# Placing and spreading the maximum units of a prompt attention's groups

## The chip, the cores and the metric

The kernel runs on one core of one Trainium2 chip. The metric is the device time of one execution in microseconds (us); the time before is the median of three runs. Engines are named as in the profile: PE is TensorE's matmuls and PEld its weight loads, DVE is VectorE, ACT is ScalarE, POOL is GpSimd, SP is SyncE, which issues most transfers.

## The reference, cut to what matters

One decoder step: projections, a paged decode attention over eight sequences, a causal prompt attention over 4096 tokens with 8 heads of 64, gates with a pooling mixer, and an output projection. What the change touches is the prompt attention:

```python
s = einsum('bqhd,bkhd->bhqk', q, k) * ATTN_SCALE
s = s + (fq[..., :, None] - fk[..., None, :])       # cumulative log-forget of query and key
s = where(k_pos[None, :] <= q_pos[:, None], s, -inf)
p = softmax(s, axis=-1)
out = einsum('bhqk,bkhd->bqhd', p, v)
```

The softmax needs the maximum of each query's row before the first exponential of that row.

## The kernel before, in words

The kernel is five phases, one behind the other: projection, decode attention, prompt attention (`phase_attend`, from 1037 to 2422 us of the profiled execution), gates, merge. The change is in `phase_attend` alone.

**Blocks and quads.** Queries are cut into tiles of 512. A block b is one head (b // 8) with one query tile (row(b) = b % 8), 64 blocks in all. Block b has row(b) + 1 quads; a quad is 512 keys against the 512 queries of the block, and the last quad of a block lies on the diagonal. There are 288 quads. A quad is two steps; a step is 256 keys: its scores are written by `scores(s, half)` in two halves, each of two matmuls (L1149, L1150), and a third small one that adds the mask on the diagonal (L1153), where the columns also narrow from 512 to 384, 256 and 128. ACT takes the exponentials of a step (`exps`, L985; on the diagonal L989, two instructions), POOL adds the probabilities up for the denominator (L951, L952, L932, L954 to L957), and PE multiplies them with v (`weigh`, L1170).

**Groups.** Three quads make a group, so there are 96 groups (numbered 0 to 95 here) of six steps and twelve halves. For each group PE's program runs the twelve halves of scores with maximum units between them, then `spread_shift` (L1130) for the blocks that start in the next group, then the six `weigh` steps (the weighing), then `total` (L1184), the denominators of blocks that ended in the group before. The score tensor `st` holds two steps, so `scores(s)` waits until the exponentials of step s - 2 are done (L1143). PE executes its program strictly in order.

**Maximum units.** The maxima are found ahead of the scores by matmuls of their own. A unit is 128 queries against up to 512 keys: one matmul (L1122) with 512 columns, or 128 to 512 on the diagonal, into one of the two banks of `mx`, then one reduction by DVE (L1048, or L1044 with the mask on the diagonal). There are 1152 units. Bank n % 2 is used again only when DVE has finished the use n - 2 (`bank_free`, L1105). When all units of a block are reduced, DVE combines them (`combine`, L1055), PE spreads the result (L1130), and ACT copies it (L967) where the scores of the block read it. DVE's order in a group is: the units that the blocks starting in the next group need, their `combine`, the other units of the group, the joins of POOL's partial sums (L1062), the denominators' copies (L1073).

**The plan.** `units_by[g]` is how many units have been issued by the end of group g. It is planned backwards from the last group: no fewer than the blocks that start in group g + 1 need plus `LATE` = 2, and no fewer than the next group's number minus `most_units(g + 1)`. `EARLY` = 14 units are issued ahead of group 0. `units_after(g, place)` says which units follow which half: place 0 is ahead of the first half, place p behind half p, so place 12 is behind the last half. In the kernel before, a group takes at most 13 units (one at each place), or 12 from group 12 on where one of its quads is on the diagonal (one at each of the places 1 to 12). The plan of before is: group 0 has 28 units, two or three at a place; 44 groups have 13; 41 have 12; the groups 9, 21, 33, ... 81 have 5 to 7; the last three groups have none.

The lines to follow are 711 to 733 (the plan), 1105 to 1124 (bank and unit on PE), 1133 to 1155 (scores), 1195 to 1211 (the order on PE), 1038 to 1048 and 1081 to 1094 (DVE's side).

```python
def bank_free(n):
    if n >= 2:
        pe.wait_ge(bank_done, n - 1)
```

Of the kernel before, what the change touches and what calls it, by code (L numbers as in the profile page):

```python
# [36 lines left out]
NT = SEQ // TILE  # L37
# [627 lines left out]
def phase_attend(nc, io, keep):  # L665
# [5 lines left out]
    LATE = 2  # L671
    QUADS = 3
    STEPS = 2 * QUADS
# [13 lines left out]
    def row(b):  # L687
        return b % NT

    quad_base = [sum(row(a) + 1 for a in range(b)) for b in range(NB + 1)]  # L690
# [7 lines left out]
    NGROUP = NQUAD // QUADS  # L698
# [3 lines left out]
    def on_diagonal(n):  # L702
        return n + 1 == quad_base[block_of[n] + 1]

    def starting(g):
        return [b for b in range(NB) if start_group[b] == g]
# [2 lines left out]
        return [b for b in range(NB) if end_group[b] == g]  # L709

    def most_units(g):
        return 4 * QUADS if g >= quad_base[NT] // QUADS and any(on_diagonal(QUADS * g + i) for i in range(QUADS)) else 4 * QUADS + 1

    units_by = [0] * NGROUP
    for g in reversed(range(NGROUP)):
        if starting(g + 1):
            units_by[g] = unit_base[starting(g + 1)[-1] + 1] + LATE
        if g + 1 < NGROUP:
            units_by[g] = max(units_by[g], units_by[g + 1] - most_units(g + 1))
        units_by[g] = min(units_by[g], unit_base[NB])  # L720
    EARLY = unit_base[starting(0)[-1] + 1] + LATE
    assert EARLY >= unit_base[starting(0)[-1] + 1]

    def units_in(g):
        return range(units_by[g - 1] if g else EARLY, units_by[g])

    def units_after(g, place):

        units = units_in(g)
        if len(units) > 2 * STEPS:  # L730
            return units[place * len(units) // (2 * STEPS + 1):(place + 1) * len(units) // (2 * STEPS + 1)]
        places = [1 + i * 2 * STEPS // len(units) for i in range(len(units))]
        return [k for k, p in zip(units, places) if p == place]

    def unit_at(k):
# [23 lines left out]

    bank_uses = [("unit", k) for k in range(EARLY)]  # L760
    for g in range(NGROUP):
# [9 lines left out]
    with ExitStack() as ctx:  # L771
# [243 lines left out]
        def _(dve):  # L1015
# [22 lines left out]
            def unit(k):  # L1038
                b, t, c = unit_at(k)
                n = bank_of["unit", k]  # L1040
                width = TILE if c < row(b) else (t + 1) * P
                dve.wait_ge(bank_ready, n + 1)
                if c == row(b):
                    nc.vector.tensor_tensor_reduce(out=mx[:, n % 2, 0:width], in0=mx[:, n % 2, 0:width], in1=tri[:, TILE - width:TILE], scale=1.0,  # L1044
                                                   scalar=NO_MAX, op0=ALU.add, op1=ALU.max,
                                                   accum_out=max_parts[:, b % AHEAD, t, c:c + 1]).then_inc(bank_done, 1)
                    return
                nc.vector.tensor_reduce(max_parts[:, b % AHEAD, t, c:c + 1], mx[:, n % 2, 0:width], AX_X, ALU.max).then_inc(bank_done, 1)  # L1048

            def combine(b):  # L1050
                h, j = head(b), row(b)
                dve.wait_ge(bank_done, bank_of["unit", unit_base[b + 1] - 1] + 1)
                if b >= 2:
                    dve.wait_ge(shift_spread, b - 1)
                nc.vector.tensor_reduce(shift_w[:, b % 2, :, HD], max_parts[:, b % AHEAD, :, 0:j + 1], AX_X, ALU.max, negate=True).then_inc(shift_ready, 1)  # L1055
# [19 lines left out]
            for b in starting(0):  # L1075
                for k in range(unit_base[b], unit_base[b + 1]):
                    unit(k)
                combine(b)
            for k in range(unit_base[starting(0)[-1] + 1], EARLY):
                unit(k)  # L1080
# [19 lines left out]
        def _(pe):  # L1100
# [9 lines left out]
            def unit(k):  # L1110
                b, t, c = unit_at(k)
                h, j = head(b), row(b)
                if k == unit_base[b]:
                    pe.wait_ge(q_loaded[b % AHEAD], (b // AHEAD + 1) * 80)
                    if j == 0 and h:
                        pe.wait_ge(bias_loaded[h % 2], (h + 1) // 2 * 16)
                    if j % 2 == 0 and h:
                        pe.wait_ge(k_loaded[h % 2][j // 2], (h + 1) // 2 * 48)
                n = bank_of["unit", k]
                bank_free(n)  # L1120
                width = TILE if c < j else (t + 1) * P
                last = nc.tensor.matmul(mx[:, n % 2, 0:width], q_top[0:KM, b % AHEAD, t * P:(t + 1) * P],  # L1122
                                        k_one[h % 2][0:KM, c * TILE:c * TILE + width], start=True, stop=True)
                last.then_inc(bank_ready, 1)
# [64 lines left out]
            pe.wait_ge(keep["k_first"], 16 * FIRST_LOADS)  # L1189
            for k in range(EARLY):  # L1190
                unit(k)
# [3 lines left out]
            for g in range(NGROUP):  # L1195
                for k in units_after(g, 0):
                    unit(k)
                for place in range(2 * STEPS):
                    scores(STEPS * g + place // 2, place % 2)
                    for k in units_after(g, place + 1):  # L1200
                        unit(k)
                if starting(g + 1):
                    pe.wait_ge(exp_done, STEPS * g + STEPS - 1)
                for b in starting(g + 1):
                    spread_shift(b, starting(g + 1)[0])
                for s in range(STEPS * g, STEPS * g + STEPS):
                    weigh(s)
                for b in dens_after(g):
                    total(b)
# [1171 lines left out]
def build(nc, io):  # L2381
    with ExitStack() as ctx:
        m = Alloc(nc, ctx, "keep")
        keep = {
            "ident": m.sb("ident", [P, P]),
            "ones": m.sb("ones", [P, P]),
            "hs_high": m.sb("hs_high", [P, KC, NS], F32R),
            "hs_low": m.sb("hs_low", [P, KC, NS], F32R),
            "f_tot": m.sb("f_tot", [H, NT]),
            "k_first": m.sem("k_first"),  # L2390
            "w_first": [m.sem("w_first0"), m.sem("w_first1")],
            "h_first": m.sem("h_first"),
            "mix_first": m.sem("mix_first"),
        }
        lane_a = nc.sbuf_base
        lane_b = lane_a + SEQ * 4
        m.sb("lanes", [P, 2 * SEQ])
        for name, lane, dt in (("project_high", lane_a, F32R), ("project_low", lane_b, F32R),
                               ("key_one", lane_a, F32R), ("key_all", lane_b, F32R),
                               ("gate_raw", lane_a, F32), ("gate_tokens", lane_b, F32), ("gate_high", lane_a, F32R),  # L2400
                               ("mix_raw", lane_b, F32), ("out_raw", lane_a, F32)):
            keep[name] = nc.alloc_sbuf_tensor_at(f"keep_{name}", [P, SEQ], dt, offset=lane)
        phase_project(nc, io, keep)
        phase_decode(nc, io, keep)
        phase_attend(nc, io, keep)
        keep["mix_s"] = m.sb("mix_s", [NS, D])
        phase_gates(nc, io, keep)
        phase_merge(nc, io, keep)
# [34 lines left out]
```

## Time and profile before

| what | value |
|---|---|
| median of three runs | 3414.8 us (3410.24 to 3417.29) |
| time of the profiled execution | 3415.05 us |
| its span in the trace | 3413.5 us |
| mean granted TensorE clock | 0.97 of full speed |
| PE matmul busy | 3228.7 us (95% of the span) |
| PE weight loads busy | 2309.1 us (68%) |
| DVE busy | 1744.9 us (51%) |
| POOL busy | 1382.8 us (41%) |
| ACT busy | 1125.5 us (33%) |

An engine's busy time is the time in which at least one of its instructions was open. Matmuls overlap in the profile: one with 512 columns is shown as 0.40 us long, while the next begins 0.23 us after it. What a matmul costs in a row of matmuls is therefore read from start to start, not from its duration. The text gives times in us from the start of the span.

### The profile page before, as it was taken

To read this page: it belongs to the slowest core of one execution; us is meant where nothing else is said; L and a number is where in the kernel's file an instruction comes from. 1 tells how busy PE (TensorE), PEld (TensorE's weight loads), DVE (VectorE), ACT (ScalarE), POOL (GpSimd) and SP (SyncE) were. 2 spreads that over 40 slices of the span, in tenths; PEclk is the share of its full clock that TensorE was granted. 3 is DMA by queue.
4 is the path that set the end of the run, shared out by engine and by line. 5 is a ranking of instruction groups with operands and counts; after the bars stand their busy time and mean duration, and the time that the engine had idled before them with its cause. 6 is when DMAs were issued, how large, how long until landed. Compare 5 with 4: busy or idle time off the path is not lost. (4 is left out here: it accounts for less than half of the span.)

```text
span 3413.5 us, 47511 instructions
## 1 busy us (share of the span) xinstructions
PE 3228.7 (95%) x16720; PEld 2309.1 (68%) x16720; DVE 1744.9 (51%) x2947; ACT 1125.5 (33%) x1536; POOL 1382.8 (41%) x1273
## 2 busy tenths in 40 slices
PE   8999999796978999999999999999799999979998
PEld 5888777672725666666666666666488888858886
DVE  4333333361515766666666666666344433554544
ACT  4222222241312555545555555554411211111011
POOL 1000000234333888888888888888500000000000
PEclk9999999897987999999999999999999999989999
DMA  5333443599996123222232323220211121167664
GB/s 183 136 137 133 142 167 120 203 358 379 366 378 138 29 53 73 60 66 60 66 66 60 70 56 70 57 80 10 96 50 51 60 86 49 49 179 218 198 203 147
DMA packets 240077, 435.55 MB, mean 128 GB/s; under 512 B 63588, under 2 KB 107717, under 8 KB 237804
## 3 DMA queue, kind: packets, MB, share of 16 engines
q1 hardware_dynamic: 216395, 358.40, 34.5%
q0 software_dynamic: 20768, 68.17, 5.2%
q10 hardware_dynamic: 2742, 6.81, 0.7%
q8 instruction: 93, 1.52, 0.2%
q14 instruction: 79, 0.65, 0.1%
HBM read 314.39 MB, written 119.08 MB: 127 GB/s over the span
## 5 line engine op out<-in xcount | busy, mean ns | idle before, releaser
L1048 DVE TENSOR_REDUCE at_max_parts<-at_mx 128x1 f32<-128x512 f32 x896 | 612.6, 691 | 165.9 <-PE at_mx L1122 151.9
L985 ACT ACTIVATE at_probs<-at_st,at_gap 128x1024 f32<-128x1024 f32 x448 | 498.4, 1115 | 376.4 <-PE at_st L1150 375.7
L951 POOL TENSOR_TENSOR at_pair_sum<-at_probs 128x1024 f32<-128x1024 f32 x224 | 537.4, 2399 | 140.9 <-ACT at_probs L985 119.0
L1170 PE MATMUL at_o_ps<-at_probs,at_v 128*64 128x512 f32 (+3 forms) x2304 | 490.6, 564 | 0.0
L1170 PEld LDWEIGHTS at_o_ps<-at_probs,at_v 128*64 128x64 f32 x2304 | 179.6, 137 | 261.7 <-issue 220.8
L952 POOL TENSOR_TENSOR at_quad_sum<-at_pair_sum 128x512 f32<-128x512 f32 x224 | 305.7, 1365 | 17.6
L93 PE MATMUL ga_acc<-keep_gate_high,ga_w_high 128*128 128x512 f32 x768 | 299.1, 389 | 0.0
L95 PE MATMUL ga_acc<-keep_gate_high,ga_w_low 128*128 128x512 f32 x768 | 299.0, 389 | 0.0
L94 PE MATMUL ga_acc<-ga_h_low,ga_w_high 128*128 128x512 f32 x768 | 298.9, 389 | 0.0
L1122 PE MATMUL at_mx<-keep_key_one,at_q_top 71*128 71x512 f32 (+2 forms) x576 | 236.2, 416 | 10.2 <-DMA at_q_one<-scratch_q_parts 5.9
L1711 POOL MEMSET mg_minus_half<- 128x1 f32 x1 | 0.6, 612 | 569.8 <-POOLq L66 569.8
L93 PE MATMUL mg_acc<-mg_w_high,mg_mix_high 128*128 128x512 f32 x512 | 202.6, 396 | 29.8 <-DVE mg_w_low L1766 23.1
L1122 PE MATMUL at_mx<-at_k_one,at_q_top 71*128 71x512 f32 (+2 forms) x576 | 227.9, 396 | 0.9 <-DVE at_den_out L1073 0.8
L1149 PE MATMUL at_st<-at_q_all,keep_key_all 128*128 128x512 f32 (+1 forms) x576 | 225.0, 391 | 1.6 <-ACT at_probs L989 0.8
L1149 PE MATMUL at_st<-at_q_all,at_k_all 128*128 128x512 f32 (+1 forms) x576 | 224.2, 389 | 2.4 <-ACT at_probs L985 1.2
L1150 PE MATMUL at_st<-at_q_one,keep_key_one 67*128 67x512 f32 (+1 forms) x576 | 221.6, 385 | 0.0
L1150 PE MATMUL at_st<-at_q_one,at_k_one 67*128 67x512 f32 (+1 forms) x576 | 219.2, 381 | 0.0
L300 POOL TENSOR_TENSOR pj_rms<-pj_squares,pj_eps_sum 128x1 f32<-128x1 f32 (+1 forms) x33 | 7.4, 224 | 491.4 <-ACT pj_junk L318 479.6
L93 PE MATMUL pj_acc<-keep_project_high,pj_w_high 128*128 128x512 f32 x512 | 202.9, 396 | 1.1 <-DVE pj_kv_rows L463 0.8
L94 PE MATMUL mg_acc<-mg_w_low,mg_mix_high 128*128 128x512 f32 x512 | 201.2, 393 | 0.0
L95 PE MATMUL mg_acc<-mg_w_high,mg_mix_low 128*128 128x512 f32 x512 | 201.1, 393 | 0.0
L95 PE MATMUL pj_acc<-keep_project_high,pj_w_low 128*128 128x512 f32 x512 | 199.6, 390 | 0.0
(337 smaller groups left out, 5734.8 us busy)
## 6 DMA issues: line engine op xcount, KB each, us to landing
dc_pages<-in_cache_k_dram SPq DMA_DIRECT2D x128, 256.0 KB, 10.7
dc_pages<-in_cache_k_dram POOLq DMA_DIRECT2D x128, 256.0 KB, 6.1
dc_pages<-in_cache_v_dram SPq DMA_DIRECT2D x128, 256.0 KB, 8.9
dc_pages<-in_cache_v_dram POOLq DMA_DIRECT2D x128, 256.0 KB, 5.5
scratch_h_t<-pj_h_t SPq DMA_DIRECT2D x8, 2048.0 KB
scratch_q_parts<-pj_stage SPq DMA_DIRECT2D x32, 512.0 KB, 3.4
scratch_k_parts<-pj_stage SPq DMA_DIRECT2D x32, 512.0 KB, 2.7
scratch_attn_t<-at_o_out SPq DMA_DIRECT2D x128, 128.0 KB, 2.4
```

What stands on the lines that cost most here:

```text
L93: nc.tensor.matmul(out, lhs_high, rhs_high, start=first, stop=False)
L94: nc.tensor.matmul(out, lhs_high, rhs_low, start=False, stop=False)
L95: return nc.tensor.matmul(out, lhs_low, rhs_high, start=False, stop=last)
L300: chain.link(nc.gpsimd.tensor_tensor(out, squares[0:rows, n:n + 1], eps_sum[0:rows], ALU.add))
L951: chain.link(nc.gpsimd.tensor_tensor(pair, first, second, ALU.add))
L952: end(n, nc.gpsimd.tensor_tensor(out, pair[:, 0], pair[:, 1], ALU.add))
L985: nc.scalar.activation(probs[:, s % RING], st[:, s % 2], ACT.Exp, bias=bias).then_inc(exp_done, 1)
L1048: nc.vector.tensor_reduce(max_parts[:, b % AHEAD, t, c:c + 1], mx[:, n % 2, 0:width], AX_X, ALU.max).then_inc(bank_done, 1)
L1122: last = nc.tensor.matmul(mx[:, n % 2, 0:width], q_top[0:KM, b % AHEAD, t * P:(t + 1) * P], k_one[h % 2][0:KM, c * TILE:c * TILE + width], ...
L1149: nc.tensor.matmul(out, k_all[h % 2][:, keys], q_all[:, b % AHEAD, at:TILE], start=True, stop=False)
L1150: last = nc.tensor.matmul(out, k_one[h % 2][0:KR, keys], q_one[0:KR, b % AHEAD, at:TILE], start=False, stop=(c < j))
L1170: last = nc.tensor.matmul(o_ps[half * HD:(half + 1) * HD, b % 2, at:TILE], v[:, h % 2, 4 * c + own], probs[:, s % RING, half, at:TILE], st ...
```

## The change

`most_units` is 14 for every group, whatever lies on the diagonal. The plan is no longer allowed to fall from one group to the next, so groups behind the last unit have none. In `units_after`, the last two units of a group (`LATE`) are put at place 12, behind the last half of the scores; the others are spread over the places from 1 on, one at a place, and only a group with more than 14 units uses the old rule.

```diff
     def most_units(g):
-        return 4 * QUADS if g >= quad_base[NT] // QUADS and any(on_diagonal(QUADS * g + i) for i in range(QUADS)) else 4 * QUADS + 1
+        return 4 * QUADS + 2

     units_by = [0] * NGROUP
     for g in reversed(range(NGROUP)):
...
         units_by[g] = min(units_by[g], unit_base[NB])
+    for g in range(1, NGROUP):
+        units_by[g] = max(units_by[g], units_by[g - 1])
     EARLY = unit_base[starting(0)[-1] + 1] + LATE
...
         units = units_in(g)
-        if len(units) > 2 * STEPS:
-            return units[place * len(units) // (2 * STEPS + 1):(place + 1) * len(units) // (2 * STEPS + 1)]
-        places = [1 + i * 2 * STEPS // len(units) for i in range(len(units))]
+        last = 2 * STEPS
+        spread = len(units) - LATE
+        if spread > last:
+            return units[place * len(units) // (last + 1):(place + 1) * len(units) // (last + 1)]
+        places = [1 + i * last // max(spread, 1) for i in range(spread)] + [last] * LATE
         return [k for k, p in zip(units, places) if p == place]
```

Worked out from these lines, the plan is now: `EARLY` stays 14; group 0 has 20 units (one or two at a place); 77 groups have 14, one at each of the places 1 to 11 and three at place 12; group 87 has 12, two of them at place 12; the groups 9, 21, 33, 45, 57, 69 and 81 have none; the groups behind these (10, 22, ... 82) have four, at the places 1, 6, 12 and 12; groups 93 to 95 have none, as before. The number of units and of all other instructions is the same.

## Rows read from the trace of the kernel before

**Rows 1.** The page: busy time of the engines over the whole span.
```profile
PE 3228.7 (95%) x16720; PEld 2309.1 (68%) x16720; DVE 1744.9 (51%) x2947; ACT 1125.5 (33%) x1536; POOL 1382.8 (41%) x1273
```
**Rows 2.** Busy by stretch: length, busy us (instructions) per engine, PEclk, DMA share, GB/s.
```profile
1400.00:1600.00 200.00, 199.50 (x1028) 129.94 (x1028) 135.69 (x248) 106.37 (x135) 173.79 (x128) 1.00 0.28 65
```
**Rows 3.** Waits from 900 to 2400 us: engine line <- releaser: us, times, longest.
```profile
ACT at_probs L985 <- PE at_st L1150: 369.8, 430, 6.4
...
POOL at_pair_sum L951 <- ACT at_probs L985: 118.9, 84, 9.1
...
PEld at_mx L1122 <- DVE at_max_parts L1048: 20.7, 95, 1.0
```
**Rows 4.** Timeline of group 31, one half: start, us, engine, line, tiles, count.
```profile
1511.05 1.39 DVE L1048 TENSOR_REDUCE at_max_parts<-at_mx 128x1 f32<-128x512 f32 x2
...
1511.32 0.40 PE L1122 MATMUL at_mx<-keep_key_one,at_q_top 71*128 71x512 f32 x1
...
1512.02 0.39 PE L1122 MATMUL at_mx<-keep_key_one,at_q_top 71*128 71x512 f32 x1
```
**Rows 5.** Timeline on PE, end of group 31, weighing, total, begin of group 32.
```profile
1516.13 0.40 PE L1122 MATMUL at_mx<-keep_key_one,at_q_top 71*128 71x512 f32 x1
1516.46 5.37 PE L1170 MATMUL at_o_ps<-at_probs,at_v 128*64 128x512 f32 x24
1521.76 0.42 PE L1184 MATMUL at_mx<-at_quad_sum,keep_ones 128*32 128x128 f32 x8
1522.12 0.50 PE L1122 MATMUL at_mx<-keep_key_one,at_q_top 71*128 71x512 f32 x1
1522.45 0.40 PE L1149 MATMUL at_st<-at_q_all,keep_key_all 128*128 128x512 f32 x1
```
**Rows 6.** Timeline, end of group 30, whose last quad is on the diagonal.
```profile
1501.50 1.29 DVE L1048 TENSOR_REDUCE at_max_parts<-at_mx 128x1 f32<-128x512 f32 x2
1501.61 0.45 PE L1122 MATMUL at_mx<-keep_key_one,at_q_top 71*128 71x512 f32 x1
...
1502.07 0.27 PE L1153 MATMUL at_st<-at_tri_t,at_ident_r 128*128 128x128 f32 x1
...
1502.25 0.33 PE L1122 MATMUL at_mx<-keep_key_one,at_q_top 71*128 71x128 f32 x1
```
**Rows 7.** Timeline, end of group 92: its last unit is needed by the spread.
```profile
2368.99 0.40 PE L1122 MATMUL at_mx<-at_k_one,at_q_top 71*128 71x512 f32 x1
...
2369.43 0.70 DVE L1044 CUSTOM_DVE_ANT_0 at_mx<-at_mx,at_tri 128x512 f32<-128x512 f32 x1
2370.05 0.14 DVE L1044 DVE_READ_ACCUMULATOR2_ANT at_max_parts<- 128x1 f32 x1
...
2370.55 0.43 PE L1130 MATMUL at_st<-at_ident_r,at_shift_w 128*65 128x128 f32 x4 [1.17 <-DVE at_shift_w L1055]
```
**Rows 8.** Stretches of groups 21, 22, 93 and 94, columns as in rows 2.
```profile
1368.50:1381.18 12.68, 12.54 (x61) 7.79 (x59) 7.54 (x13) 6.84 (x9) 11.97 (x10) 1.00 0.09 21
1381.18:1395.39 14.21, 14.21 (x70) 8.39 (x70) 9.86 (x19) 6.68 (x6) 13.01 (x9) 1.00 0.16 38
...
2376.22:2388.21 11.99, 11.07 (x54) 6.70 (x52) 1.38 (x2) 6.62 (x9) 11.24 (x10) 1.00 0.10 23
2388.21:2400.84 12.63, 12.15 (x58) 5.95 (x57) 0.00 (x0) 6.36 (x6) 11.93 (x8) 1.00 0.00 0
```
**Rows 9.** Timeline on ACT, group 94: two exponentials a row.
```profile
2389.46 2.12 ACT L985 ACTIVATE at_probs<-at_st,at_gap 128x1024 f32<-128x1024 f32 x2 [3.96 <-PE at_st L1150]
2391.88 2.12 ACT L985 ACTIVATE at_probs<-at_st,at_gap 128x1024 f32<-128x1024 f32 x2 [0.30 <-PE at_st L1150]
```
**Rows 10.** Stretches of group 0: scores part and weighing, columns as in rows 2.
```profile
1055.69:1079.40 23.71, 22.86 (x64) 16.86 (x64) 16.85 (x35) 6.11 (x10) 7.72 (x9) 0.50 1.00 196
1079.40:1086.50 7.10, 7.10 (x25) 3.45 (x24) 0.42 (x2) 1.18 (x2) 2.04 (x3) 0.62 0.71 157
```
**Rows 11.** Timeline on PE, group 0: units behind each other.
```profile
1066.81 0.79 PE L1122 MATMUL at_mx<-keep_key_one,at_q_top 71*128 71x512 f32 x1 [0.65 <-DVE at_max_parts L1048]
...
1067.83 0.63 PE L1150 MATMUL at_st<-at_q_one,keep_key_one 67*128 67x512 f32 x1
...
1068.26 0.63 PE L1122 MATMUL at_mx<-keep_key_one,at_q_top 71*128 71x512 f32 x1
```

## The prediction

> **What bounds the kernel now.** The page's busy shares come first: PE is open for 95% of the span, no other engine for more than 51% [rows 1]. The stretches show what that means in the prompt attention: from 1400 to 1600 us PE is busy for 199.5 of 200 us at a granted clock of 1.00, POOL for 174, DVE for 136, ACT for 106 [rows 2]. The waits agree: ACT waits for scores (369.8 us), POOL waits for ACT (118.9 us), while PE's waits for DVE's reductions are 20.7 us in 95 places [rows 3]. So PE's order and its own waits set the time, every microsecond that PE stands still in this phase is a microsecond of the kernel, and slack on DVE or POOL is worth nothing by itself.
>
> The margin is thin in one place. In group 31 a unit starts every 0.70 us on PE (1511.32, 1512.02), which is two matmuls of scores and one unit at 0.234 each; DVE's two reductions there take 1.39 us, 0.695 each [rows 4]. A unit that comes once per half is just kept up with. Behind the group's last unit (1516.13) the weighing starts 0.33 later and lasts to 1521.76 [rows 5]; DVE has no units in that time.
>
> **The change, part by part.** No instruction is added or removed. Units move: 8 out of group 0, and out of the groups 9, 21, ... and 10, 22, ...; 77 groups now have 14. In these, three units stand behind each other at place 12.
>
> *The three units in a row.* Let T be the start of the first. The unit before it started at T - 0.70. DVE takes a unit up 0.44 behind its start (2368.99 to 2369.43 [rows 7]), so it reduces that one from T - 0.26 to T + 0.43. The second unit needs that bank. PE starts a waiting unit 0.06 behind the end of the reduction: in group 30 the first of two reductions ends near 1502.19 (half a pair of 1.29, its own length being 0.69), and the unit starts at 1502.25, where the mask's matmul before it began at 1502.07 and takes 0.06 [rows 6]. So the second unit starts at T + 0.49 instead of T + 0.23: 0.25 lost. The third needs the bank of the first, which is reduced from T + 0.44 to T + 1.13: it starts at T + 1.19, instead of 0.23 behind the second: 0.48 lost. Together 0.73 per group. Nothing covers this, since the weighing, which would not need these banks, is queued behind the units on PE. 77 x 0.73 = 56.2, and 0.25 in group 87 with its two: **+56.5**. The bounds: 0 if the wait were hidden in some way that the rows do not show, and 0.9 per group if DVE comes late to T. A part of the units is narrow (the mean is 469 of 512 columns), which takes a little off.
>
> *DVE late at the diagonal.* In 38 of the 77 groups the last quad is on the diagonal, halves are shorter than a reduction there, and DVE is already behind when place 12 comes: the units at 1501.61 and 1502.25 are 0.64 apart, and the second of them had waited [rows 6]. Between 0 and 0.2 each; the few hundredths by which that unit was late are the nearest, 0.07 x 38 = **+2.7**.
>
> *The spread.* Where a starting block needs all but two units of the group, its last needed unit is now the first of the three. From such a unit to the spread it takes 1.56 us (2368.99 to 2370.55, with a reduction on the diagonal of 0.76) [rows 7]; the third unit starts near T + 1.25 there and is over by T + 1.4 to 1.5, so the spread waits for 0.1 to 0.2 more. This is so in 16 groups; in 8 of them the plan of before ended as tight and waited already, elsewhere the need had been met long before. **+2**, between 0 and 4.
>
> *Groups with few units.* Without units, scores outrun ACT. In group 94, which has none, exponentials start every 1.21 us (two in 2.42: 2389.46 to 2391.88 [rows 9]), and PE needs four matmuls, 0.94, for a step; from the third step on PE waits about 0.27 each. Units that stood there ran for free. Groups 9, 21, ... 81 get none: group 93, of the same shape, takes 11.99 where group 21 takes 12.68 with seven units of 2816 columns [rows 8], which are 1.29 of matmul time; the units gone should have saved 1.29 and save 0.69, a loss of 0.60. Groups 10, 22, ... 82 keep four of 13, of which one stands where it fills a wait (place 6), one comes ahead of the second half and delays the first exponentials, and two come last: 4 x 0.27 - 0.23 = 0.85 lost, where group 22 has no such waits (PE busy 14.21 of 14.21 [rows 8]). 7 x (0.60 + 0.85) = **+10.1**. Between 5 and 14.
>
> *Place 0.* A unit ahead of the first half is gone. The first matmul behind the weighing takes 0.33 to the next one, a unit or not (1522.12 to 1522.45 [rows 5]; the weighing starts likewise 0.33 behind the last unit). No gain: 0.
>
> *Group 0.* It loses 8 units (3968 columns), which are paid later at the full clock with 3968 x 0.234 / 512 = **+1.8**. The scores part of group 0 takes 23.71 us at a clock of 0.50, the lower level of 1.2 GHz, and the weighing 7.10 at 0.62 [rows 10]; there a matmul of 512 columns costs 0.43 (1067.83 to 1068.26), and the second of two units waits for DVE (the one at 1066.81: 0.65 idle) [rows 11]. Eight units less are 8 x 0.41 = 3.3, and most of the waits between doubled units go, about 1.9: 5.2 less. But the clock rises inside the weighing. If it rises at the same moment as before, the work that moves ahead of it runs at half speed, and only half of 5.2 is kept; if it rises at the same place of the program, all. **-3.5**; bounds -2.6 and, if a PE with fewer gaps got the full clock from group 0's begin on (23.7 to about 14 us for 20 reductions), -12.
>
> *Cover.* The joins on DVE (1.6 us, at most two) start some 0.1 us later relative to the weighing and still end inside it. SP's loads of q and k wait on scores and on groups that are all later, and need no more room. Other phases are not touched.
>
> The sum: 56.5 + 2.7 + 2 + 10.1 + 1.8 - 3.5 = 69.6, on the profiled execution's 3415.05 (span 3413.5 and 1.5 around it; 0.25 over the median): **3484.5 us**, 2% more.
>
> **What a page says of the clock.** In group 92 PE stood idle for 1.17 us ahead of the spread [rows 7], and the stretches behind it (groups 93, 94) still have a granted clock of 1.00 [rows 8]; so I put no loss of clock into the sum. The Trainium skill (TensorE: Matmul & The Clock Gate, "A second HAM failure mode: psum-queue depth-cycling") says that a PE which micro-idles between groups of matmuls while it cycles through PSUM banks can swing between the two clock levels. That speaks against this change, which adds such a gap to 77 groups; by that rule the time would be that of the clock rival below, the trace with its one gap does not agree, and it has no repeated gaps to show.
>
> **The rivals.**
> - *The clock falls at the gaps.* For it: the gap comes back every 15 us, and group 0, with its waits for DVE, never got the full clock in its scores part. Against it: group 92. Price: a matmul costs 0.43 instead of 0.234 [rows 11], 13 us of such a group would take 11 us more; if one in ten of the 77 groups were hit, 85 us more, 3570.
> - *The wait is partly covered.* If DVE came to the first of the three earlier than I read, or narrow units were luckier, half of 56.5 is lost: 3456.
> - *Faster.* The mechanism is DVE's lead at the diagonal. In before, some 47 of the 96 groups have diagonal halves shorter than a reduction, and PE waits for DVE inside them [rows 6]; a group that begins with scores and whose doubled units lie in front of the weighing would keep DVE ahead, if the last two units cost PE nothing. It decides at place 12: the waits must be absent there. Then at most the 20.7 us of waits [rows 3] go, and group 0 gives 3.5: 3391. Against it: two banks, and 0.69 for each reduction.
> - *Nothing to see.* If POOL set the pace (174 of 200 us), PE's waits would be absorbed, and ACT's loss too: 3415. Against it: POOL itself waits for ACT.
>
> **How the numbers follow.** The forecast has 0.82, the partly covered wait 0.06, the clock 0.06, faster 0.03, nothing 0.03. The range takes the forecast's bounds (-12 for group 0 and some 14 off the three units below; 0.2 per diagonal group, 4 for the thin groups and a few short falls of the clock above) and reaches to the partly covered case: 3458 to 3500. A change of 0.2%, 6.8 us, is about what a measurement of this kernel can tell from none: faster 0.03, same 0.03, slower 0.94.
>
> **What would show it.** In the timeline on PE: three L1122 at the end of a group, 0.49 and 0.7 apart, and the weighing 1.5 behind the first. In the waits: PE or PEld at L1122 for DVE L1048 up from 20.7 to about 75 us. Groups 9, 21, ... near 12.0 us, groups 10, 22, ... near 13.3, groups with 14 units near 15.2 where 13 took 14.4. The clock at 1.00 from group 1 to the end of the phase. I am wrong if the three units stand 0.23 apart, or if the phase's stretches show a clock below 1.00.

## The result and the profile after

The changed kernel takes 3486.61 us (median of four runs, 3482.32 to 3490.21) beside 3413.49 of the kernel before (also four runs, 3410.24 to 3417.29): a ratio of 1.0211, interval 1.0199 to 1.0223, 2.1% slower. Forecast were 3484.5 and a range of 3458 to 3500. The profiled execution took 3490.21 us (span 3488.6), 75.2 more than that of before.

The busy line of the page stands beside [rows 1]:

```profile
PE 3272.3 (94%) x16720; PEld 2311.6 (66%) x16720; DVE 1734.0 (50%) x2947; ACT 1123.8 (32%) x1536; POOL 1382.6 (40%) x1273
```

PE is open for 43.6 us more with the same 16720 matmuls: two that overlap less are open longer, and that is no added work. Stretches of the changed kernel show more (columns as in [rows 2]). In order they are: the stretch of [rows 2]; the middle of the phase; the scores part and the weighing of group 0 ([rows 10]); groups 21 and 22 ([rows 8]); group 31, where a unit came every 0.70 us in [rows 4]; and group 93 ([rows 8]):

```profile
1400.00:1600.00 200.00, 195.25 (x966) 120.43 (x967) 125.37 (x232) 96.43 (x117) 167.57 (x120) 1.00 0.24 54
...
1100.00:2400.00 1300.00, 1267.14 (x6190) 783.03 (x6189) 820.77 (x1490) 629.34 (x757) 1068.12 (x760) 0.99 0.25 57
...
1053.51:1072.02 18.51, 18.51 (x56) 15.05 (x56) 11.46 (x25) 6.11 (x10) 6.77 (x8) 0.50 0.96 184
1072.02:1078.77 6.75, 6.75 (x26) 3.29 (x25) 0.53 (x1) 1.19 (x2) 2.98 (x4) 0.65 1.04 226
1381.63:1393.61 11.98, 11.06 (x54) 6.70 (x52) 0.83 (x1) 6.62 (x9) 11.25 (x10) 1.00 0.10 23
1393.61:1406.92 13.31, 13.03 (x62) 6.70 (x61) 4.13 (x8) 6.58 (x6) 12.31 (x9) 1.00 0.16 40
...
1527.88:1543.22 15.34, 15.06 (x72) 8.59 (x71) 12.13 (x18) 7.29 (x7) 12.57 (x9) 1.00 0.22 53
...
2449.27:2461.25 11.98, 11.06 (x55) 6.71 (x53) 1.39 (x2) 6.61 (x9) 8.37 (x8) 1.00 0.10 23
```

PE was busy for 199.5 of 200 us and now is for 195.25. Group 31 takes 15.34 us with 14 units. Group 21 has no units any more and takes what group 93 takes (11.98); group 22 takes 13.31. And from 1100 to 2400 us the granted clock is 0.99, not 1.00.

The waits from 900 to 2473 us of the changed kernel; the third line answers to the last of [rows 3], which was 20.7 us in 95 places:

```profile
ACT at_probs L989 <- PE at_st L1154: 365.0, 396, 7.4
POOL at_pair_sum L955 <- ACT at_probs L989: 173.6, 81, 7.5
...
PEld at_mx L1126 <- DVE at_max_parts L1052: 63.6, 161, 1.0
...
PE at_mx L1126 <- DVE at_max_parts L1052: 18.0, 72, 0.6
```

PE and PEld together wait 81.6 us for DVE's reductions at L1052, where the forecast had about 75. POOL waits for ACT for 173.6 us instead of 118.9: it has more slack now. The end of group 31, which answers to [rows 5], on PE, and then DVE's reductions of the same time:

```profile
1535.95 0.98 PE L1126 MATMUL at_mx<-keep_key_one,at_q_top 71*128 71x512 f32 x2
1537.13 0.50 PE L1126 MATMUL at_mx<-keep_key_one,at_q_top 71*128 71x512 f32 x1 [0.19 <-DVE at_max_parts L1052]
1537.56 5.37 PE L1174 MATMUL at_o_ps<-at_probs,at_v 128*64 128x512 f32 x24
...
1543.22 0.50 PE L1153 MATMUL at_st<-at_q_all,keep_key_all 128*128 128x512 f32 x1
```

```profile
1535.69 2.67 DVE L1052 TENSOR_REDUCE at_max_parts<-at_mx 128x1 f32<-128x512 f32 x4 [0.19 <-PE at_mx L1126]
1538.28 1.77 DVE L1066 TENSOR_TENSOR at_quad_sum<-at_quad_sum 128x512 f32<-128x512 f32 x1
```

The first row holds the first two of the three units. A matmul of 512 columns that follows a gap is shown 0.50 long, so the second began at 1535.95 + 0.98 - 0.50 = 1536.43, 0.48 behind the first. The third began at 1537.13, 1.18 behind the first, and DVE finished a reduction every 0.67 in that time. Without waits they would stand 0.23 apart. The idle time in brackets is only 0.19, because it counts from the modelled end of a matmul; the distance of the starts is what is lost. The weighing begins 0.43 behind the last unit, where [rows 5] had 0.33.

**The sum of the groups.** Taken from start to start, the 96 groups are 74.6 us longer in the profiled execution. What a group takes over its matmuls at 0.234 us for 512 columns is its excess. A thin group is one with no or only four units, and a fall is a short stretch in which the granted clock is at its lower level (shown further below). The parts are:

| part | forecast | measured |
|---|---|---|
| 77 groups of 14 and group 87: three in a row, diagonal, spread | 56.5 + 2.7 + 2 = 61.2 | 62.0 |
| 7 groups without units | 4.2 | 3.7 |
| 7 groups with four units | 5.9 | 7.4 |
| 8 units moved out of group 0 | 1.8 | 1.8, not measured apart |
| group 0 | -3.5 | -5.6 |
| falls of the clock in five weighings | 0 | 8.0 |
| ends of eight groups (-2.1) and the last group (-0.6) | 0 | -2.7 |
| sum | 69.6 | 74.6 |

### The profile page after: what moved, and what is told of

Its sections match the earlier page's. It is cut to its first block and busy times, and to the rows that moved or that the text cites. A ratio compares the mean times of both kernels' runs of the same rounds, so it can differ in the third digit from the quotient of the medians.

```text
span 3488.6 us, 47511 instructions
## 1 busy us (share of the span) xinstructions
PE 3272.3 (94%) x16720; PEld 2311.6 (66%) x16720; DVE 1734.0 (50%) x2947; ACT 1123.8 (32%) x1536; POOL 1382.6 (40%) x1273
## 5 line engine op out<-in xcount | busy, mean ns | idle before, releaser
L1052 DVE TENSOR_REDUCE at_max_parts<-at_mx 128x1 f32<-128x512 f32 x896 | 605.1, 690 | 178.9 <-PE at_mx L1126 169.8
L955 POOL TENSOR_TENSOR at_pair_sum<-at_probs 128x1024 f32<-128x1024 f32 x224 | 536.5, 2395 | 196.1 <-ACT at_probs L989 173.6
L1174 PE MATMUL at_o_ps<-at_probs,at_v 128*64 128x512 f32 (+3 forms) x2304 | 498.2, 572 | 0.0
L956 POOL TENSOR_TENSOR at_quad_sum<-at_pair_sum 128x512 f32<-128x512 f32 x224 | 294.3, 1314 | 17.6
L1126 PE MATMUL at_mx<-keep_key_one,at_q_top 71*128 71x512 f32 (+2 forms) x576 | 236.1, 418 | 20.4 <-DVE at_max_parts L1052 9.2
L1126 PE MATMUL at_mx<-at_k_one,at_q_top 71*128 71x512 f32 (+2 forms) x576 | 230.3, 404 | 13.5 <-DVE at_max_parts L1052 8.8
```

Of the source, the lines that this page charges most:

```text
L955: chain.link(nc.gpsimd.tensor_tensor(pair, first, second, ALU.add))
L956: end(n, nc.gpsimd.tensor_tensor(out, pair[:, 0], pair[:, 1], ALU.add))
L1174: last = nc.tensor.matmul(o_ps[half * HD:(half + 1) * HD, b % 2, at:TILE], v[:, h % 2, 4 * c + own], probs[:, s % RING, half, at:TILE], st ...
```

## The experiments

Theory A is the forecast's: PE waits for DVE's reduction of the bank two units back, and the weighing is queued behind. The kernel before was measured again beside them, with medians between 3415.9 and 3417.0 us.

**e1_old_places.** The new plan with the old places:

```diff
-        last = 2 * STEPS
-        spread = len(units) - LATE
-        if spread > last: ...
-        places = [1 + i * last // max(spread, 1) for i in range(spread)] + [last] * LATE
+        if len(units) > 2 * STEPS:
+            return units[place * len(units) // (2 * STEPS + 1):(place + 1) * len(units) // (2 * STEPS + 1)]
+        places = [1 + i * 2 * STEPS // len(units) for i in range(len(units))]
```

> The plan of the changed kernel (77 groups of 14 units), but with the places of before: one unit at each of the places 0 to 11 and two at place 12. Theory A (the cost is the wait for two banks at the end of a group): only the second unit of the pair waits, 0.25 us instead of 0.73, so the 77 groups lose some 19 us instead of 56 and the time is about 3487 - 37 = 3450 us, a few less if falls of the clock go as well (3438 to 3454). The thin groups stay as slow as in the changed kernel. Rival B (the cost is the plan itself, full groups and thin groups, wherever the units stand): the time stays within 8 us of 3487.

Measured: 3449.43 us, ratio 1.0093 (1.0072 to 1.0114). As theory A has it: half of the loss (37 us of 73) was where the units stood, with the counts of all groups unchanged. The rest is mainly the pair at place 12 (0.36 in each of 77 groups) and the thin groups (9 us).

**e2_old_plan.** The old plan with the new places:

```diff
     def most_units(g):
-        return 4 * QUADS + 2
+        return 4 * QUADS if g >= quad_base[NT] // QUADS and any(on_diagonal(QUADS * g + i) for i in range(QUADS)) else 4 * QUADS + 1
```

> The plan of before (12 and 13 units, group 0 with 28), but the new places: the last two units of a group at place 12, the others from place 1 on. Theory A: one wait of 0.25 us in 85 groups, 21 us, and a few for doubled places: 3414 + 24 = 3438 us (3432 to 3446). Rival B (the plan alone costs): within 6 us of 3414. With e1 this also says what the third unit at place 12 costs over the second: by theory A it is twice as dear (0.48 against 0.25).

Measured: 3449.46 us, ratio 1.0094 (1.0076 to 1.0111), 33 us over before and not 24; the range of 3432 to 3446 was missed. The places alone cost, so rival B is out, but each of the 85 groups lost 0.38 us and not 0.25. The missing 0.1 is read in the starts. A unit of 512 columns that had to wait is followed by the spread 0.34 us later, where it was 0.24 without a wait, and by the weighing 0.43 us later, where it was 0.33. The excess of the changed kernel's groups has this cost too, once for each group.

**e3_narrow_tail.** DVE's time alone, PE's program untouched. The two reductions that the last units wait for read 128 columns, so these maxima are over fewer keys:

```diff
+    narrow = {k for g in range(1, NGROUP) if len(units_in(g)) > 2 * STEPS for k in units_in(g)[-4:-2]}
...
                 width = TILE if c < row(b) else (t + 1) * P
+                at = width - P if k in narrow else 0
...
-                nc.vector.tensor_reduce(..., mx[:, n % 2, 0:width], AX_X, ALU.max)
+                nc.vector.tensor_reduce(..., mx[:, n % 2, at:width], AX_X, ALU.max)
```

> The changed kernel, but the two reductions for which the last two units of a group wait (the unit at place 11 and the first at place 12) read only the last 128 of their columns; the maximum of these units is then taken over fewer keys. PE's program is the same to the instruction. Theory A: the second unit no longer waits, the third waits from T + 0.47 to T + 0.44 + 0.29 + 0.06 = T + 0.79, 0.32 us; the tail costs 0.32 instead of 0.73, 77 x 0.41 = 32 us less: about 3455 us (3445 to 3462), with L1126's idle for DVE falling from 99 to about 67 us. Rival B (three matmuls into the same bank pair cost PE this however long DVE takes): 3487.

Measured: 3456.52 us, ratio 1.0119 (1.0101 to 1.0136), 30 less than the changed kernel. With the same order on PE and only DVE faster, the loss shrinks by about what the arithmetic of the three starts says: the groups with 14 units have 0.36 less excess each, where 0.41 was expected. The end of group 29 of this kernel on PE:

```profile
1493.28 0.62 PE L1129 MATMUL at_mx<-keep_key_one,at_q_top 71*128 71x512 f32 x2
1494.06 0.50 PE L1129 MATMUL at_mx<-keep_key_one,at_q_top 71*128 71x512 f32 x1 [0.16 <-DVE at_max_parts L1055]
```

The first two units now stand 0.23 apart, and the third is 0.78 behind the first; expected was 0.79. So the wait is for the reductions. PE's idle time at L1126 for them, diagonal ones included, fell from 99.3 to 59.2 us.

**e4_units_in_weighing.** The last two units behind the first step of the weighing, where both banks are free:

```diff
-        places = [...] + [last] * LATE
+        places = [...] + [last if needs_all(g) else last + 1] * LATE
...
                     weigh(s)
+                    if s == STEPS * g:
+                        for k in units_after(g, 2 * STEPS + 1):
+                            unit(k)
```

> The changed kernel, but the last two units of a group stand behind the first step of the weighing instead of at place 12 (group 92, where the spread needs all, stays as it is). The first step takes 0.88 us, so both banks are free when PE comes to them. Theory A: the tail's 56 us go, the diagonal's 3 and most of the falls of the clock too (8 us): 3487 - 65 = 3422 us (3415 to 3435, the upper end if DVE's joins, now some 2 us later in the weighing, hold up the totals). The thin groups keep their 11 us, group 0 its gain. Rival B: units cost what they cost, 3487. Rival C (a switch between the matmul kinds costs some 0.1 us each way, 0.2 per group): 3437.

Measured: 3473.03 us, ratio 1.0163 (1.0146 to 1.018). A clear miss, by 51 us. On PE, the end of group 14 of this kernel:

```profile
1284.57 0.43 PE L1139 MATMUL at_st<-at_ident_r,at_shift_w 128*65 128x128 f32 x4 [1.15 <-DVE at_shift_w L1064]
1284.93 1.08 PE L1179 MATMUL at_o_ps<-at_probs,at_v 128*64 128x512 f32 x4
1285.93 0.73 PE L1131 MATMUL at_mx<-at_k_one,at_q_top 71*128 71x512 f32 x2
1286.60 4.51 PE L1179 MATMUL at_o_ps<-at_probs,at_v 128*64 128x512 f32 x20
```

The two units (third row) wait for nothing, as expected, but two things had been overlooked. The switch into the units and back costs 0.35: the weighing is 0.81 longer for 0.47 of units. This comes in 84 groups, the thin ones with four units among them, and makes 29 us (rival C had 15 for it). And in 15 groups the plan ends just two units ahead of the need. There the last needed unit is now directly ahead of the spread, which waits for its reduction and the combine. The bracket in the first row is this wait; from start to start it is 1.54, of which 1.3 is lost, 20 us in all. In the changed kernel the two further units had covered this. The profiled execution, at 3482.05 the longest of the four, also has two falls of the clock, in groups 2 and 92, each 6.8 us long; the one in group 2 made its weighing 3.3 us longer.

**e7_weighing_margin.** The same with a wider margin in the plan:

```diff
-            units_by[g] = unit_base[starting(g + 1)[-1] + 1] + LATE
+            units_by[g] = unit_base[starting(g + 1)[-1] + 1] + 2 * LATE
```

> As e4 (the last two units of a group behind the first step of the weighing), but the plan keeps four units ahead of what a starting block needs instead of two, so the last needed unit is no longer at place 12 ahead of the spread. In e4 the spread waited 1.35 us in 16 groups, and the other groups of 14 units were 0.5 us shorter than in the changed kernel. Theory A (e4 lost its gain to these waits for the spread): 16 x 1.3 = 21 us less than e4's 3473, so 3452, with two more units in group 0: 3450 (3443 to 3458). Rival (something else in the weighing holds e4 up): 3473.

Measured: 3453.71 us, ratio 1.0103 (1.0087 to 1.0118). So e4's second loss was the spread. The rest of the distance to the kernel before is mainly the switch (29 us) and the thin groups; units inside the weighing do not beat one unit per half.

**e6_lead_alone.** The shorter lead in the kernel before:

```diff
     def most_units(g):
+        if 1 <= g <= 8:
+            return 4 * QUADS + 2
```

> The kernel before, with the shorter lead alone: groups 1 to 8 take 14 units instead of 13 (places of before, so two at place 12), and group 0 so has 20 instead of 28. All later groups are as before. Theory A: group 0 gains 5.6 us, as in the changed kernel, the eight units cost 1.8 us later, and the pairs at place 12 cost 8 x 0.35 = 2.8 us: 1 us faster, which the times cannot show (3409 to 3417 beside 3414); the profile should show group 0 at about 25.3 us instead of 30.8 and groups 1 to 8 some 0.6 longer each. Rival: the full clock comes earlier and group 0 gains 10 us or more: 3404.

Measured: 3419.2 us, ratio 1.0002 (0.9993 to 1.0012), eleven runs. No difference, as expected. Group 0 and groups 1 to 8, as stretches of this kernel:

```profile
1056.53:1080.49 23.96, 23.96 (x79) 17.73 (x80) 12.00 (x25) 7.30 (x12) 9.76 (x11) 0.57 1.01 195
1080.49:1199.40 118.91, 117.54 (x581) 73.80 (x581) 81.74 (x149) 57.97 (x66) 95.31 (x65) 1.00 0.19 48
```

Group 0 is 23.96 instead of 30.81 ([rows 10]: 23.71 + 7.10), and the eight groups behind it took 114.11 before and take 4.80 more. 6.85 gained, 4.80 given back, 2 us left in one profile: less than the times can tell.

**e5_four_in_a_row.** The last four units of a group at place 12:

```diff
-        spread = len(units) - LATE
-        if spread > last:
+        spread = len(units) - 2 * LATE
+        if len(units) - LATE > last:
...
-        places = [1 + i * last // max(spread, 1) for i in range(spread)] + [last] * LATE
+        places = [1 + i * last // max(spread, 1) for i in range(max(spread, 0))] + [last] * min(2 * LATE, len(units))
```

> The changed kernel, but the last four units of a group are put at place 12 behind the last half instead of the last two: with 14 units one place (6) is empty and four units stand in a row. Theory A (each further unit in a row waits for a reduction, 0.69 + 0.06 less its own 0.234): the fourth waits 0.46 more, 77 x 0.46 = 35 us, and the seven groups with four units now have all of them in a row and wait some 1.2 each, 8 us: 3487 + 43 = 3530 us (3522 to 3545). Clock: the profile of the changed kernel shows four falls of the granted clock in groups with three in a row; if the falls come with the length of the gaps, there are more of them here (each 1.7 us), if they were chance, none or as many. Rival B (a fixed price for having units behind the scores, whatever their number): 3487.

Measured: 3592.08 us, ratio 1.0508 (1.049 to 1.0526), 105 over the changed kernel and not 43, a miss. The waits are what theory A says: the excess of the scores parts grew by 51 us (0.46 in a group without a diagonal, 0.63 where the last quad is on it, 1.18 in the groups with four units). The weighings are 43.5 us longer than the changed kernel's (51.5 longer than with no fall at all), and there is the clock. The other 6 us of the 100.7 between the two profiled executions lie outside the groups. Stretches of e5: most of the phase, then two that begin with a weighing:

```profile
1100.00:2500.00 1400.00, 1349.10 (x6241) 796.65 (x6240) 800.35 (x1507) 635.99 (x764) 1066.64 (x762) 0.96 0.24 54
1453.90:1457.30 3.40, 3.40 (x13) 1.79 (x14) 3.10 (x5) 0.59 (x1) 3.24 (x5) 0.51 0.02 5
1471.00:1474.40 3.40, 3.40 (x11) 1.47 (x13) 1.16 (x2) 0.59 (x1) 3.24 (x5) 0.50 0.02 6
```

The mean clock of the phase is 0.96, which is made of the full clock and of short pieces at the lower level, 0.5. The granted clock over the whole span is 0.952 to 0.958 in all four executions of e5; the kernel before has 0.968 to 0.973 beside them. The first of the two weighings follows this end of a row on PE, two units in each of the first two rows:

```profile
1452.28 0.98 PE L1126 MATMUL at_mx<-keep_key_one,at_q_top 71*128 71x512 f32 x2
1453.57 1.19 PE L1126 MATMUL at_mx<-keep_key_one,at_q_top 71*128 71x512 f32 x2 [0.30 <-DVE at_max_parts L1052]
1454.56 0.64 PE L1134 MATMUL at_st<-at_ident_r,at_shift_w 128*65 128x128 f32 x4
```

**e8_four_narrow.** As e5, with the three reductions that units in the row wait for narrowed to 128 columns, in the way of e3 (`[-5:-2]` instead of `[-4:-2]`).

> As e5 (four units in a row), but the three reductions for which units in the row wait (the unit at place 11 and the first two at place 12) read only the last 128 of their columns, so their maxima are over fewer keys; PE's program is that of e5. In e5 the weighings of 30-odd groups ran in part at the lower clock, some 52 us. Theory A (the lower clock follows the length of PE's gaps ahead of the weighing): the row's waits shrink from 1.2 to some 0.4 us, 77 x 0.8 = 62 us, the falls go with them, 52 us, together 3592 - 114 = 3478 us (3465 to 3490), with at most 4 falls in the phase. Rival B (the falls come from the order of PE's work, so many units in a row ahead of the weighing, whatever the gaps): the falls stay, 3530 us.

Measured: 3475.29 us, ratio 1.017 (1.0153 to 1.0187). Same program on PE, 117 us less. In the groups' sum of the profile 58.3 us of it are waits and 50.7 us are weighings at the full clock again; its phase has one fall of the clock, where e5's has 33, and the clock from 1100 to 2400 us is 1.00:

```profile
1100.00:2400.00 1300.00, 1271.84 (x6258) 784.71 (x6258) 753.12 (x1512) 637.59 (x768) 1076.98 (x765) 1.00 0.25 58
```

The four executions have a granted clock of 0.969 to 0.974. So the falls came with the longer waits and not with the order of the work, which is the same in both kernels.

**e9_changed_again.** The changed kernel itself, for a second profile.

> The changed kernel once more, for a second profile. If the falls of the clock inside the phase belong to the kernel, there are again some two to six of them in groups with three units in a row, each 1.7 us; if they were chance of one execution, none.

Measured: 3487.41 us in one execution, with two falls in the phase (one in group 92). Its groups are the same as in the first profile to 0.02 us in the mean, but for the weighings, which are 5.3 us shorter together. How many falls there are is thus not the kernel's alone: five in one execution, two in the other.

## The clock, across the runs

A fall looks like this in the changed kernel: group 6's units, spread and weighing on PE, and the stretch behind the weighing's start.

```profile
1164.07 1.13 PE L1126 MATMUL at_mx<-keep_key_one,at_q_top 71*128 71x512 f32 x2 [0.15 <-DVE at_max_parts L1052]
1165.04 0.40 PE L1134 MATMUL at_st<-at_ident_r,at_shift_w 128*65 128x128 f32 x4
1165.37 6.63 PE L1174 MATMUL at_o_ps<-at_probs,at_v 128*64 128x512 f32 x24
```

```profile
1165.30:1168.80 3.50, 3.50 (x12) 1.00 (x11) 0.63 (x1) 0.59 (x1) 3.42 (x4) 0.52 0.02 5
```

The stretch is at 0.52, the lower level of 1.2 GHz, and the weighing takes 6.63 us where another group's of the same shape (`x24` with a diagonal) takes 4.94: 1.7 us a fall. The table counts the falls in groups 1 to 94, one profiled execution for each kernel but the changed one. The lost time is the excess of a group without a diagonal over the kernel before:

| kernel | lost per group, us | falls |
|---|---|---|
| before | none | 0 |
| e6 (pair at place 12 in eight groups) | 0.4 in those | 0 |
| e1, e2 (two at place 12) | 0.4 | 0 and 1 |
| e3 (three, narrow) | 0.5 | 1 |
| e4 (two inside the weighing) | 0.4; 1.5 in 15 groups, with the spread's wait | 2, twice as long |
| e7 (as e4, without that wait) | 0.3 | 1 |
| changed kernel, two executions | 0.9 | 5 and 2 |
| e5 (four) | 1.3 | 33 |
| e8 (four, narrow) | 0.6 | 1 |

The single falls in e2, e3, e7 and e8 are all in group 92, where the spread waits over 1.1 us in each kernel. That wait alone does not settle it: before, e1 and e6 have it too and no fall there. The first of e4's two falls is in group 2, behind one of its long waits for the spread. And the lost time of a group is not the whole condition either: in e5, 25 of the 38 groups of 14 units whose last quad is on the diagonal had a fall and 6 of the 32 without a diagonal, with the same 1.3 to 1.4 us lost. The runs leave open why. The Trainium skill (TensorE: Matmul & The Clock Gate, "A second HAM failure mode: psum-queue depth-cycling") says that micro-idles of PE between groups of matmuls, as it cycles through PSUM banks, can make it swing between its two clock levels. The runs agree: this kernel had few falls with 0.9 us lost per group of 15 us, and many with 1.3.

## Why the prediction was right, point by point

- *PE bounds the phase.* Right. Group times went up by PE's lost time and nothing absorbed it; POOL and ACT only waited longer.
- *Three units in a row, 0.73.* Right in place and nearly in size. The starts stand 0.48 and 1.18 behind the first, forecast 0.49 and 1.19. Not in the sum was the 0.10 behind a waiting matmul: groups without a diagonal lost 0.86. The diagonal term (+0.07) had the wrong sign: groups with the last quad on the diagonal lost 0.73, less than the others. They had waits in their last halves before ([rows 6]), which would explain it; no run shows this by itself. Together it is 62.0 for 61.2.
- *Spread, +2.* The trace shows next to nothing of it. In every group from 1 to 91 that has a spread and 14 units, it starts 0.31 to 0.34 behind the third unit, so it does not wait; in group 92 it starts 1.67 behind, where it was 1.56. e4 shows what covers it: with the two units gone, the spread starts 1.54 behind the last unit. That the three terms together came out near their sum, 62.0 for 61.2, is thus partly luck: the spread's 2 us and the diagonal's 2.7 were not there, and the 0.10 behind the waiting matmul, 8 us over 77 groups, stood in their place.
- *Groups with few units, 10.1.* Measured 11.1. Group 21 at 11.98 and group 22 at 13.31 are the forecast's 12.0 and 13.3. That ACT's pace is the bound there is supported by the equality with group 93, not by an experiment of its own.
- *Place 0, nothing.* A small gain was missed. In the kernel before, behind each of the eight groups that total two denominators, the next group's unit at place 0 waited for DVE's copy of the first (at 1269.75: 0.20 idle, ended by L1073), because the copy frees its bank. With no unit at place 0 the next matmul starts 0.27 sooner, 2.1 us over the eight. e1, which keeps a unit at place 0, does not have the gain; e2 has it.
- *Group 0, -3.5.* Measured -5.6: its scores part went from 23.71 to 18.51, as the 5.2 said, and the full clock came 23.2 us behind the start of its scores instead of 29.1, so all of it was kept in this pair of profiles. Whether the clock follows the program is not shown, because the moment of its rise varies from execution to execution: e2, whose group 0 has the 28 units and the 23.7 us of before, had the full clock after 25.7 us and took 29.12 for the group instead of 30.81. Against e2 the gain is 3.9; e6 has 6.85, with the full clock after 20.6 us. So the forecast's half is neither confirmed nor refuted.
- *The clock at the gaps, nothing in the sum.* This is the step that failed: the sum has nothing for the clock, on the ground that group 92 kept the full clock behind its one gap. The falls cost 8.0 us in the profiled execution and 3.1 in the second. The ground itself was one execution's: the same wait in group 92 is followed by a fall in both executions of the changed kernel and in e2, e3, e4, e5, e7 and e8. By the forecast's own sign it was wrong here: it named a clock below 1.00 in the phase, and the stretch from 1100 to 2400 us is at 0.99. The rival had this mechanism, with 0.06. Its price for one in ten groups (85 us) was far too high, since a fall costs 1.7 us and not a whole group at the lower level; e5 had 33 falls for 52 us.

The rows behind two of these points are the unit at place 0 in the kernel before, with its wait, and e2's group 0 as one stretch:

```profile
1269.75 0.50 PE L1122 MATMUL at_mx<-at_k_one,at_q_top 71*128 71x512 f32 x1 [0.20 <-DVE at_den_out L1073]
...
1053.07:1082.19 29.12, 28.28 (x86) 19.49 (x86) 17.28 (x36) 7.30 (x12) 9.75 (x11) 0.56 0.95 198
```

The errors, +8.0 for the clock, +1.0 for the thin groups, +0.8 for the row, -2.1 for group 0, -2.7 for the ends of groups and the last group, partly cancel to 5.0. That 3484.5 and the median of 3486.61 are only 2 us apart is luck to that extent; the profiled execution took 3490.21. The faster rival (units at the end cost nothing) and the one in which POOL sets the pace are excluded by the result, and by e3, where shorter reductions of DVE alone gave 30 us back.

No version that was run beats the kernel before. e6 equals it. With one unit per half, PE brings a unit every 0.70 us and DVE needs 0.69: 13 units are what a group takes without a wait, and each further one costs a wait (e1), a switch (e7) or a thin group elsewhere.

## What to carry to other kernels

When two engines pass buffers at nearly the same pace, count the instructions in a row per buffer: with two banks and a reduction of 0.69 us, the second unit in a row lost 0.25 us, and the third and the fourth nearly 0.5 each, however idle the reducing engine is afterwards. Everything queued behind them in order waits too. A bank that becomes free during the next stage is no help if its user stands ahead of that stage. And price a repeated gap on PE twice, once for itself and once for the clock: here the step from three to four units in a row cost 51 us of waits and 44 us of weighings at the lower clock.

## What the runs showed of the hardware that was not expected

- A matmul of 512 columns that waited is followed 0.10 us later than one that did not: by the spread after 0.34 instead of 0.24 us, by the weighing after 0.43 instead of 0.33 (e2: 0.38 lost per group, 0.25 of it the wait).
- The granted clock fell with short gaps that recur: 5 and 2 times with 0.9 us lost in each of 77 groups and 33 times with 1.3. With 0.6 or less it fell only behind a wait of over 1.1 us for the spread, in group 92 and once in group 2 of e4. A fall 3.4 us long cost 1.7 us, one of 6.8 us in e4 cost 3.3.
- Two units between steps of the weighing cost 0.35 us over their own 0.47, though nothing waited (84 times in e4, and again in e7).
